# Weight sums by accumulating DMAs, plain blocks' low parts on VectorE, and an earlier second norm in a two-block decoder kernel

## What is computed

```python
def swiglu(h, wg, wu, wd):
    return (jax.nn.silu(h @ wg) * (h @ wu)) @ wd
...
x = x + 0.5 * swiglu(rms_norm(x, ffn1_norm[l]), ffn1_wg[l], ffn1_wu[l], ffn1_wd[l])   # D_MODEL 1024, D_FF 2816
...
x = x + memory_cross_attention(rms_norm(x, mem_x_norm[l]), ...)
x = x + 0.5 * swiglu(rms_norm(x, ffn2_norm[l]), ffn2_wg[l], ffn2_wu[l], ffn2_wd[l])
```

## Time and profile before

| | |
|---|---|
| median of 3 runs | 1880.97 us (1880.72 to 1883.0) |
| profiled execution, device time | 1880.62 us |
| its span, first to last instruction | 1878.7 us |
| TensorE busy | 1834.4 us, 98% |
| VectorE busy | 1154.5 us, 61% |
| ScalarE busy | 771.3 us, 41% |
| GpSimd busy | 485.7 us, 26% |
| bytes moved by DMA | 145.49 MB |

### The profile page before, as it was taken

One profiled execution on the slowest core, in us unless ns is written; L12 is line 12 of the kernel. 1 busy time (PEld: TensorE's weight loads), 2 busy tenths in 40 slices (PEclk: granted clock), 3 DMA queues, 4 the chain that ended last, 5 costly groups with the idle time before them and its releaser, 6 DMA issues. The chain is left out here.

```text
span 1878.7 us, 29611 instructions
## 1 busy us (share of the span) xinstructions
PE 1834.4 (98%) x12020; PEld 1633.4 (87%) x12020; DVE 1154.5 (61%) x1669; ACT 771.3 (41%) x1392; POOL 485.7 (26%) x330
## 2 busy tenths in 40 slices
PE   8999999999999999899999999999999998999999
PEld 8999888979988887899988877989768878999887
DVE  7533465655416667899974555646557488999531
ACT  4112454321226544444433314445565554444321
POOL 5443211454341123100034423310004331000343
PEclk9999999999999999999999999999999999999999
DMA  4222100223220012332323233200003223323232
GB/s 164 96 83 90 35 12 12 79 96 96 80 90 2 23 53 82 116 117 94 102 74 101 90 118 115 80 24 1 1 1 124 79 68 117 116 95 102 68 101 102
DMA packets 41048, 145.49 MB, mean 77 GB/s; under 512 B 5072, under 2 KB 5328, under 8 KB 40784
## 3 DMA queue, kind: packets, MB, share of 16 engines
q1 hardware_dynamic: 40912, 143.59, 22.9%
HBM read 140.40 MB, written 2.10 MB: 76 GB/s over the span
## 5 line engine op out<-in xcount | busy, mean ns | idle before, releaser
L453 POOL TENSOR_TENSOR wl<-raw,wh 128x1024 fp32r<-128x1024 f32 (+1 forms) x178 | 431.2, 2423 | 1022.6 <-ACT wh L445 1022.4
L445 ACT ACTIVATE wh<-raw 128x1024 fp32r<-128x1024 f32 (+1 forms) x178 | 188.7, 1060 | 596.0 <-PE ps L459 524.4
L457 PE MATMUL ps<-xh,wh 128*128 128x264 f32 (+3 forms) x1144 | 384.6, 336 | 13.5 <-POOL wl L453 10.8
L458 PE MATMUL ps<-xl,wh 128*128 128x264 f32 (+3 forms) x1144 | 380.9, 333 | 0.0
L459 PE MATMUL ps<-xh,wl 128*128 128x264 f32 (+3 forms) x1144 | 380.3, 332 | 0.0
L457 PE MATMUL ps<-XSh,wh 128*128 128x256 f32 (+1 forms) x864 | 285.4, 330 | 8.9 <-DVE wl L1743 6.0
L459 PE MATMUL ps<-XSh,wl 128*128 128x256 f32 (+1 forms) x864 | 284.5, 329 | 0.0
L458 PE MATMUL ps<-XSl,wh 128*128 128x256 f32 (+1 forms) x864 | 284.4, 329 | 0.0
L457 PEld LDWEIGHTS ps<-xh,wh 128*128 128x128 f32 x1144 | 215.1, 188 | 43.0 <-issue 18.8
L458 PEld LDWEIGHTS ps<-xl,wh 128*128 128x128 f32 x1144 | 215.3, 188 | 22.3 <-issue 1.0
L459 PEld LDWEIGHTS ps<-xh,wl 128*128 128x128 f32 x1144 | 215.4, 188 | 21.9
(11 more groups left out here) (420 smaller groups left out, 3470.7 us busy)
## 6 DMA issues: line engine op xcount, KB each, us to landing
raw<-wstream SPq DMA_DIRECT2D x176, 512.0 KB, 3.3
rawx<-wpairs SPq DMA_DIRECT2D x44, 512.0 KB, 3.5
raw<-wpairs SPq DMA_DIRECT2D x24, 512.0 KB, 3.5
raw<-wstream SPq DMA_DIRECT2D x10, 528.0 KB, 3.4
h<-xT SPq DMA_DIRECT2D x4, 528.0 KB, 6.0
out<-h SPq DMA_DIRECT2D x8, 256.0 KB, 4.2
HF<-wpairs SPq DMA_DIRECT2D x2, 512.0 KB, 4.3
xs<-wpairs SPq DMA_DIRECT2D x2, 512.0 KB, 5.9
```

Source lines behind the costliest of these rows:

```text
L445: e.activation(wh[p % 2][:, 0:n], raw[c % 2][:, 0:n], ACT.Copy).then_inc(*w_hi(p))
L453: e.tensor_tensor(wl[p % 2][:, 0:n], raw[c % 2][:, 0:n], wh[p % 2][:, 0:n].bitcast(F32), ALU.subtract).then_inc(*w_lo(p))
L457: e.matmul(o, w_h, x_h, start=start, stop=False)
L458: e.matmul(o, w_h, x_l, start=False, stop=False)
```

## The change

Four edits:
1. The four sums of each pair are no longer additions of VectorE. GpSimd issues a DMA for each that adds its source to its destination (`accum_op`). Sum a is made in the buffer of quarter 21, b in the same buffer behind the split of a, c in the buffer of quarter 11 behind b (its source is quarter 21 again, from HBM), d in the buffer of 21 behind the split of b. GpSimd issues all 36 of a stage one after the other. A pair now needs four buffers: `homes` puts the next pair's quarter 22 where this pair's 11 lies, and its 12 where this 12 lies.
2. The low weight parts of the plain chunks g2, u2, g3 and u3 are made by VectorE (`split_lo_dve`) instead of GpSimd.
3. VectorE's and ScalarE's programs in the plain blocks are written in another order.
4. The second feed-forward's norm is summed behind tile g0 instead of u0, and its squares stand in the last loop of the memory attention.

```diff
+V_SPLIT = {(st + part, f) for st in ("ffn1", "ffn2") for part in "gu" for f in range(2, PLAIN)}
...
-            at = [{"11": 0, "21": 1, "a": 6, "22": 7, "12": 8}, {"11": 2, "21": 3, "22": 0, "12": 1, "a": 4, "spare": 5}]
+            at = [{"11": 0, "21": 8, "22": 7, "12": 1}, {"11": 2, "21": 3, "22": 0, "12": 1}]
             while len(at) < PAIRS:
...
+                a, b = at[-2:]
+                old = {"11": 4, "21": 5} if len(at) == 2 else {"11": a["21"], "21": a["22"]}
+                at.append({**old, "22": b["11"], "12": b["12"]})
...
-        HOLDS = {"11": "11", "12": "12", "22": "22", "a": "a", "b": "11", "c": "21", "d": "12"}
+        HOLDS = {"11": "11", "12": "12", "22": "22", "a": "21", "b": "21", "c": "11", "d": "21"}
...
-            part = {"11": "b", "12": "d", "21": "c", "22": "22", "a": "a"}[role]
+            part = {"11": "c", "12": "12", "21": "d", "22": "22"}[role]
...
+        def split_lo_dve(e, on, p):
+            c = CHUNK[PARTS[p]]
+            on.wait_ge(*w_hi[p])
+            e.tensor_tensor(wl[p % 2][:, 0:1024], raw[c % 2][:, 0:1024], wh[p % 2][:, 0:1024].bitcast(F32),
+                            ALU.subtract).then_inc(*s_lo(*PARTS[p]))
...
             if name == "a":
                 on.wait_ge(*pair_loaded(st, u, "21"))
                 on.wait_ge(*pair_loaded(st, u, "22"))
...
+                dst, more = of["21"], of["22"]
+            elif name == "b":
+                on.wait_ge(*pair_loaded(st, u, "11"))
+                on.wait_ge(*s_hi[st, u, 1])
+                on.wait_ge(*s_lo[st, u, 1])
+                dst, more = of["21"], of["11"]
             elif name == "c":
...
+                on.wait_ge(*pair_summed(st, "b", u))
                 on.wait_ge(*s_hi[st, u, 0])
                 on.wait_ge(*s_lo[st, u, 0])
...
+                dst, more = of["11"], wpairs[u + (0 if st == "ffn1" else PAIRS), 1]
             else:
...
+                on.wait_ge(*pair_loaded(st, u, "12"))
+                on.wait_ge(*s_hi[st, u, 3])
+                on.wait_ge(*s_lo[st, u, 3])
+                dst, more = of["21"], of["12"]
+            e.dma_start(dst, more, accum_op=ALU.add).then_inc(d_sum[name], 16)
...
-                if i == 1:
-                    pair_sum(e, on, st, u, "d")
...
-                if u + 1 < PAIRS and i in (3, 5, 6):
-                    pair_sum(e, on, st, u + 1, {3: "a", 5: "c", 6: "b"}[i])
...
-                    if f == 0 and s == 1 and st == "ffn2":
+                    if f == 0 and s == 0 and st == "ffn2":
                         norm_pe(e, on, st, T, 1, pair(st), SUMMED(st))
...
         def ffn_pool(e, on, st):
-            for f in range(PLAIN - 1):
-                split_lo(e, on, PART[st + "g", f] + 2)
-                split_lo(e, on, PART[st + "u", f] + 2)
+            split_lo(e, on, PART[st + "g", 1])
+            split_lo(e, on, PART[st + "u", 1])
+            for u in range(PAIRS):
+                for name in "abcd":
+                    pair_sum(e, on, st, u, name)
...
                     gained_hi(e, on, "ffn2", m, h[:, m, M:L], P_("g_ffn2", m, m + 1), xh[:, m, M:L], v_out["mo", m])
+                    square(e, on, "ffn2", m, h[:, m, M:L], [], slot_free("ffn2", m, {0: [], 1: [], 2: []}))
             split_hi(e, on, PART["mo", 1] + 2)
-            for m in range(KT):
-                square(e, on, "ffn2", m, h[:, m, M:L], [], slot_free("ffn2", m, {0: [], 1: [], 2: []}))
...
+                    add_square(e, on, "ffn2", m - 1, T)
...
-            for m in range(KT):
-                add_square(e, on, "ffn2", m, T)
```

More of the change, by code:

```diff
@@ L1679, in low @@
                     *v_lo(st, "x", i))
[L1681 to L1710, removed]
-            yield
+            def normal_rows(first):
+                for k in range(first, first + 4):
+                    gain = gg[:, k:k + 1] if st == "ffn1" else P_("g_ffn2", k, k + 1)
+                    e.scalar_tensor_tensor(normal[:, k, :], h[:, k, M:L], gain, r, ALU.mult, ALU.mult).then_inc(
+                        *x_norm(st, "n", k))
@@ L1968, in ffn_dve, with scaled_out @@
             on.wait_ge(*scaled)
-            steps = mixed_dve(e, on, st)
-            for f in range(PLAIN):
+            normal_rows, low, turn_ = mixed_dve(e, on, st)
+            def scaled_out(f):
                 b = bank[st, f]
@@ L1979, in ffn_dve, with product @@
                     *v_out(st, "up", f))
+            def product(f):
                 on.wait_ge(*v_out[st, "up", f])
                 on.wait_ge(*a_out[st, "silu", f])
-                if f == 0:
-                    for s in early_room(st):
-                        on.wait_ge(*s)
                 e.tensor_tensor(hidden(f), xb[:, f % 2, 0:T], tmpn[:, f % 2, 0:T], ALU.mult).then_inc(
                     *v_out(st, "gated", f))
-                for _ in range((2, 2, 1, 0)[f]):
-                    next(steps, None)
-                if f == 2:
-                    for name in "acb":
-                        if name == "b":
-                            pair_low(e, on, st, 0)
-                        pair_sum(e, on, st, 0, name)
+            scaled_out(0)
+            for s in early_room(st):
+                on.wait_ge(*s)
+            normal_rows(0)
+            product(0)
+            turn_(1)
+            low(0)
+            split_lo_dve(e, on, PART[st + "g", 2])
+            normal_rows(4)
+            low(1)
+            scaled_out(1)
+            turn_(3)
+            split_lo_dve(e, on, PART[st + "u", 2])
+            low(2)
+            turn_(4)
+            product(1)
+            split_lo_dve(e, on, PART[st + "g", 3])
+            low(3)
+            turn_(6)
+            scaled_out(2)
+            low(4)
+            split_lo_dve(e, on, PART[st + "u", 3])
+            product(2)
+            low(5)
+            low(6)
+            pair_low(e, on, st, 0)
+            scaled_out(3)
             pair_low(e, on, st, 1)
             pair_low(e, on, st, 2)
+            product(3)
             pairs_dve(e, on, st)
```

74 lines of the change are left out of this document (44 added, 30 removed).

## The result

The changed kernel takes 2005.3 us (median of 4 runs, 2001.9 to 2008.0) against 1881.0 in the same session: 1.0657 times before, interval 1.0637 to 1.0678. The direction was forecast, the size was not: 1921 was predicted and the range ended at 1994. The profiled execution took 2007.33 us.

The account below looks back on a forecast made before the run. TensorE, busy 1834.4 of 1878.7 us, was taken as the bound. From 1880.6 us, 9.6 gained in plain blocks and second norm and 50.0 lost to the pairs' ring gave 1921.0 us; range 1868 to 1994.

Parts of the forecast that it names:

- Plain blocks, first stage: First feed-forward stage before the pairs: low parts on VectorE start the first pair product at 763.8 instead of 769.81, gaining 6.0 us.
- Second norm: Second feed-forward stage: up 0 starts 3.5 us late, later blocks recover it, first pair product comes earlier; gain 3.6 us.
- the walk: Step-by-step pricing of the plain blocks' new order; in the second stage it starts up block 0 3.5 us late.
- What the plain waits cost: TensorE's waits for low parts in both stages' plain blocks, the only prizes: 7.4 + 8.3 = 15.7 us at most.
- the 44 us of idle time: Whole kernel before: TensorE idles 44 us, so no edit can be worth more than that.
- Unloading VectorE is worth nothing: Pairs: VectorE is busy 162 of 180 us but TensorE doesn't wait for it, so removing 36 additions a stage gains 0.
- The ring, and that latency sets the pace: Pairs: dependences b, c, split c, load 22, a, split a take 3L + 8.4 us against 20.04; 50.0 us lost; chance 0.57.
- the DMA engines as such set the changed kernel's pace: Rival, pairs: sums add 12 us of transfers, engines 0.9 busy, each sum queues behind a load; 1994 us, chance 0.14.
- L taken 4.8: Pairs: L, a sum's time from release to landing, taken as 4.8 us like the 1024 KB load.
- the load at 3.6: Pairs: loading the next pair's quarter 22 takes 3.5 us, 3.6 with its wake-up.
- The upper bound of L, 6.2: Pairs: a sum's landing with one more transfer in front of it, 4.8 + 1.4 = 6.2 us.
- The Trainium skill's fit: GpSimd's DMAs take 2.0 us + bytes / 436 GB/s: 3.2 us for 512 KB written, 4.4 with both operands; not used in the sum.

Follow-up runs that it names:

- experiment 13: The kernel of 1 (sums on VectorE, other edits kept) with the second norm and its squares back in their old place: 1868.8 us, 0.992 of before.
- Experiment 14: The kernel of experiment 13 with VectorE again taking the last end tile before the k block's two low parts: 1866.1 us, 0.9923 of before.
- 1: The changed kernel with all four sums of each pair made by VectorE again, all other edits kept: 1868.7 us, 0.9931 of before.
- 2: The changed kernel with one more 512 KB buffer, so loading the next 22 no longer waits for c; all sums stay DMAs: 1924.9 us, 1.0224 of before.
- 6: The kernel of 2 (one buffer more) with sum b made by VectorE right behind the low part of a: 1871.1 us.
- Experiment 10: The changed kernel with the load of quarter 12, and the loads queued behind it, held back until sum a has landed: 1991.3 us.
- experiment 4: The changed kernel with the sums' DMAs only copying, the addition left out, so the output is not the reference's: 1921.6 us.
- 12: As 1, but sum d is an accumulating DMA and VectorE makes c and b in slots 4 and 5: 1867.2 us, 0.9927 of before.
- 7: The kernel of 2 (one buffer more) with sum a made by VectorE, in slot 5: 1967.6 us.
- 8: The kernel of 7 with VectorE's sum a issued two slots earlier, in slot 3: 1940.5 us.

## Why the prediction was right in direction and wrong in size

- **Plain blocks, first stage: right.** 6.55 us gained (769.81 to 763.26), forecast 6.0. The waits at g2, g3 and u3 are gone; u2's is 1.69, forecast 2.1.
- **Second norm: right.** 3.8 us gained in the second stage (59.64 from the first addition to `h` to the first pair product, against 63.47), forecast 3.6. u0 starts 18.6 us behind that addition (15.0 before); the walk had 3.5 more than before. The gain is not the new norm's: experiment 13 shows that this edit taken alone costs 1.4, where the walk had some 2.4 (6.0 against 3.6).
- **What the plain waits cost: too low.** They were priced at their own length. The last of them, 2.81 us ahead of the first product, also lowered the clock behind it, and at 0.50 TensorE still counts as busy, so the 44 us of idle time are no bound of what an edit can gain. This row is of the kernel before:

```profile
772.00:774.00 2.00, 2.00 (x11) 2.00 (x11) 1.65 (x3) 2.00 (x3) 0.00 (x0) 0.50 0.00 0
```

  Experiment 14 has that wait no longer but the end of the pairs as before, and its pairs take 182.3 and 182.1 us instead of 183.8: 1.5 and 1.7 us a stage, which fits the lowered clock.
- **Unloading VectorE is worth nothing: right** for the kernel before. With all sums back on it (1) TensorE is busy without a gap.
- **The ring, and that latency sets the pace: right.** Taking the sums out (1) brings the time back, and cutting the ring by a buffer (2) brings back 80 us of 137. That the DMA engines as such set the changed kernel's pace is excluded by 2 and 6: both move the transfers faster (shares of 0.72 and 0.74 against 0.62) and are faster, and in 6 nothing waits from 800 to 900. That rival's price was good all the same: it put 12 us of engine time on four sums, and they take 11.2 (2.8 each).
- **What failed is the term "L taken 4.8", and with it the load at 3.6.** L was priced for a sum that has the DMA engines for itself, and one value served three sums. So b is indeed 4.8. But c, whose source lies in HBM, is 5.4; the load of 22 is 4.25; and a is 7.9, because the split of c releases the load of 22 and the three loads queued behind it within some 4 us (833.83 to 838.09), and a goes out at their end, at 838.08. Experiment 10 and each stage's last pair show that this burst is the cause: without it a takes 4.6. The turn above, step by step, forecast then measured: split c 2.4, 2.46; load 3.6, 4.25; a 4.8, 7.85; split a 2.4, 3.02; b 4.8, 4.82; c 4.8, 5.42. That is 22.8 and 27.8. With the mean turns of 27.70 and 27.75, eight turns make 39.2 and 39.6 us more than forecast, 79 of the 86 us between forecast and profile.
- The upper bound of L, 6.2, did allow for "one more transfer in front". As a mean that covers the 6.0 found here ((7.85 + 4.82 + 5.42) / 3). But it was attached to the rival in which the engines are full all the time, with a small chance. The mean share is 0.62; the engines are full only while the burst lasts, and a goes out just then:

```profile
836.00:838.00 2.00, 2.00 (x14) 2.00 (x14) 2.00 (x4) 0.86 (x1) 0.00 (x0) 0.71 1.02 414
838.00:840.00 2.00, 2.00 (x19) 2.00 (x19) 1.97 (x4) 0.00 (x0) 0.85 (x1) 1.00 1.05 297
```

  The last two figures are the DMA share and GB/s. (The view adds up packets' times, so a full stretch can come out a little above 1.)
- **The other 7.5 us** of the 86 are a sum of errors that partly cancel. The split of a stage's first c starts 2.1 and 3.4 us later behind the first product than its term had it (777.38 - 763.26 = 14.1 where 12.0 was put), and from the last c's split to the k block it is 12.9 and 12.8 (999.00 to 1011.92), where three products and a split were put at 11.0; some of those products run at the lower clock (below). Together that is 9.3. Against it stand 6.7, because the pairs before took 183.8 a stage and not the 180.4 that was subtracted, and 0.8 more gain in the plain blocks. Some 6 us lie outside these stretches, 4.1 of them the wait for ScalarE's `XSh`. That wait belongs to the order at the end of the pairs, an edit that the prediction did not price (14); in the kernels whose pairs don't wait it is 2.1 to 2.5.
- **The Trainium skill's fit** (DMA: Bandwidth & Descriptors, "Anatomy of one DMA — SWDGE (gpsimd) path") gives 3.2 us for 512 KB. The plain copies from SBUF of experiment 4 agree, 2.9 to 3.1 for b with its wake-up; the accumulating DMA doesn't, 4.55. Counted with both operands it gives 4.4, close to that b, though not to any sum that shares the engines.

Left open: the 1.5 us that an accumulating b costs over a copy match the 1.4 us more for which a sum keeps the engines busy; whether that is the second read or the addition itself no run here separates. Nor does a run show whether four such sums a pair can keep up with TensorE once every ring is cut. The best kernels found, experiments 1 and 12 to 14, are equal within what the runs can tell: 0.992 to 0.993 of before. They share edits 2 and 3; no run separates these two.

## What to carry to other kernels

When work moves from a busy engine to DMAs, write down every cycle of dependences that the new latency closes, through buffers and through the order of each engine's queue, and compare it with the work per turn; here three different rings of 20.9 to 27.7 us against 20.04 paced the slow kernels. One buffer undid the first, one sum back on VectorE the second, one slot of order the third. Price a transfer on such a ring by what is released together with it, not by the row of an undisturbed one. A step that is "off the ring" stays off only as long as nobody in a queue waits behind or ahead of it. And when two paths meet, read which one ends last: product c looked like a member of the second ring, but VectorE's queue beside it ended later, and only that explains what experiments 7 and 8 cost.

## What the runs showed of the hardware

- An accumulating DMA of 512 KB, from GpSimd's issue to the start of the engine that waits for it: 4.55 us from SBUF, 5.4 with its source in HBM; plain copies 3.06 and 3.70. Among four loads sum a took 5.9 to 9.2 in the changed kernel, a copy in its place 4.7 to 7.5; without them 4.6 and 2.9 to 3.0.
- An accumulating DMA of 512 KB keeps the 16 DMA engines busy for 2.8 us, a copy issued by GpSimd for 1.4 (experiment 4; by the time that their packets took, which neighbours may stretch).
- GpSimd spends 0.85 us on issuing an accumulating DMA and 0.53 on a copy.
- A stall can cost TensorE more than itself. Windows of experiment 2 around the fourth row shown there:

```profile
846.50:848.80 2.30, 0.05 (x1) 0.01 (x1) 1.36 (x2) 1.79 (x2) 0.00 (x0) 1.00 1.05 208
848.80:849.70 0.90, 0.88 (x7) 0.90 (x8) 0.90 (x1) 0.89 (x1) 0.00 (x0) 1.00 1.07 214
849.90:852.90 3.00, 3.00 (x16) 3.00 (x15) 2.92 (x4) 1.87 (x2) 0.00 (x0) 0.50 1.01 369
853.30:856.00 2.70, 2.70 (x25) 2.70 (x25) 2.67 (x5) 1.06 (x1) 0.00 (x0) 1.00 0.94 293
```

After 2.3 us without matmuls the clock is granted in full for about 1 us, then at 0.50 (1.2 GHz of 2.4) for 3 us, in which 16 matmuls run where 28 would have; product c takes 4.6 us instead of 2.86. Not every wait did this: behind the 1.69 us ahead of u2 the clock stayed at 1.00 (720 to 763.30 in the changed kernel). The mean clock of 0.92 and the same number of matmuls fit TensorE's busy time in the changed kernel's pairs, 201 us a stage instead of some 180. What the lower clock costs there in time isn't shown: the ring doesn't pass through TensorE, and in experiment 2 product c still ends 1.9 us before VectorE takes it. In the kernel before, some 1.6 us a stage fit it (above).
